# Stick-breaking attention of four heads: values projected together, the next head's queries and keys between the items, diagonal items on fewer columns

## The reference, cut to what matters

```python
q, k, v = [t.reshape(bsz, s, SB_HEADS, SB_HEAD_DIM) for t in jnp.split(qkv, 3, axis=-1)]   # qkv = h @ w_in
q, k = rms_norm_2(q, q_norm_g), rms_norm_2(k, k_norm_g)
# for blocks of 128 queries and 128 keys, from the diagonal outwards (o = 0, 1, ...):
z = jnp.einsum("bhnqd,bhnkd->bhnqk", qb[:, :, o:], kb[:, :, :n])     # qb is scaled by d ** -0.5
log_beta = jax.nn.log_sigmoid(z)
log_keep = log_beta - z
if o == 0: log_keep = jnp.where(diag_mask, log_keep, 0.0)
after = jnp.einsum("bhnqj,js->bhnqs", log_keep, suffix) + acc[:, :, o:, :, None]
att = jnp.exp(log_beta + after)
if o == 0: att = jnp.where(diag_mask, att, 0.0)
out = out.at[:, :, o:].add(jnp.einsum("bhnqk,bhnkd->bhnqd", att, vb[:, :, :n]))
acc = acc.at[:, :, o:].add(jnp.sum(log_keep, axis=-1))
```

## Time and profile before

| | us |
|---|---|
| median of 3 runs | 5148.59 (5147.55 to 5153.25) |
| profiled execution, its time | 5148.16 |
| profiled execution, its span | 5146.3 |
| the stage of the change, from its first load to the next stage's | 2812.3 to 3272.3 |

### The profile page before, as it was taken

The page is one execution under the profiler, slowest core; times in us unless marked ns, Lnnn a source line. Parts: engine busy times, 40 slices in busy tenths (PEclk is TensorE's granted clock), DMA queues, the critical chain, the costliest instruction groups (busy, mean ns, idle before and its releaser), DMA issues. The chain is left out here.

```text
span 5146.3 us, 45404 instructions
## 1 busy us (share of the span) xinstructions
PE 4150.6 (81%) x17034; PEld 2982.0 (58%) x17034; DVE 2160.6 (42%) x2568; ACT 1483.9 (29%) x2331; POOL 890.4 (17%) x386
## 2 busy tenths in 40 slices
PE   6698699978696899777667888874699875799996
PEld 6576455557574455555446555553477764566663
DVE  0293366632463676322374111315212202566665
ACT  1211245531112445210313333312210101455551
POOL 0142300002343000023110111120234322100001
PEclk6799799989898899888888998986799985899997
DMA  4111112222111021123221101220233230799995
GB/s 147 57 37 31 31 65 83 74 84 96 33 43 39 25 68 55 62 78 37 38 49 45 13 12 12 23 26 0 25 43 49 31 131 35 280 379 380 379 346 217
DMA packets 351721, 470.70 MB, mean 91 GB/s; under 512 B 46301, under 2 KB 217282, under 8 KB 351042
## 3 DMA queue, kind: packets, MB, share of 16 engines
q1 hardware_dynamic: 338770, 423.88, 28.4%
q0 software_dynamic: 7888, 26.78, 1.4%
q10 hardware_dynamic: 4896, 17.83, 0.9%
HBM read 396.59 MB, written 71.86 MB: 91 GB/s over the span
## 5 line engine op out<-in xcount | busy, mean ns | idle before, releaser
L1089 PE MATMUL values<-probs,vp 128*128 128x512 f32 x672 | 348.9, 601 | 12.0 <-issue 6.4
L1178 ACT ACTIVATE probs<-scores 128x512 f32<-128x512 f32 (+1 forms) x336 | 196.1, 584 | 309.2 <-PE scores L211 307.5
L1387 POOL TENSOR_TENSOR out_hi<-out_w,ones 128x1024 fp32r<-128x1024 f32 x24 | 57.3, 2388 | 1197.6 <-DMA out_w<-in_w_out 1197.6
L209 PE MATMUL scores<-q_hi,k_rest 97*128 97x512 f32 (+1 forms) x336 | 262.4, 781 | 0.0
L676 DVE SCALAR_TENSOR_TENSOR conv_out<-conv_in,vectors,conv_out 128x1295 f32<-128x1295 f32 (+1 forms) x120 | 254.3, 2119 | 4.3
L2927 PE MATMUL dp<-h_t,abt 128*128 128x512 f32 x544 | 241.9, 597 | 1.9 <-ACT abt L2975 1.9
L209 PE MATMUL gates_ps<-x_t_r,gates_w_r 128*128 128x512 f32 (+1 forms) x560 | 210.3, 376 | 22.0 <-POOL gates_w_r L257 22.0
L209 PE MATMUL out_ps<-h_t_r,out_w_r 128*128 128x512 f32 (+1 forms) x448 | 172.2, 384 | 67.8 <-POOL out_w_r L1389 67.8
L2957 ACT ACTIVATE expert_hi<-wu 128x1024 fp32r<-128x1024 f32 x136 | 144.9, 1065 | 253.2 <-PE gp L211 253.2
L1260 DVE TENSOR_REDUCE mx<-made 128x1 f32<-128x640 f32 (+1 forms) x272 | 203.6, 793 | 27.1 <-PE made L1030 26.5
L210 PE MATMUL gates_ps<-h_t_r,gates_hi 128*128 128x512 f32 (+1 forms) x560 | 209.9, 375 | 0.0
(11 more groups left out here) (517 smaller groups left out, 10247.6 us busy)
## 6 DMA issues: line engine op xcount, KB each, us to landing
wg<-in_w_gate SPq DMA_DIRECT2D x34, 2048.0 KB, 10.1
wu<-in_w_up SPq DMA_DIRECT2D x34, 2048.0 KB, 11.7
h_t<-in_w_down SPq DMA_DIRECT2D x34, 2048.0 KB, 10.1
slot_rows<-zero_rows SPq DMA_DIRECT2D x16, 1536.0 KB, 9.7
ahead_w<-in_w_ada SPq DMA_DIRECT2D x48, 512.0 KB, 3.8
slot_rows<-yb ACTq DMA_DIRECT2D x34, 512.0 KB, 8.1
gates_w<-in_w_in SPq DMA_DIRECT2D x28, 512.0 KB, 3.9
mod_w<-in_w_mod SPq DMA_DIRECT2D x12, 1024.0 KB, 5.1
```

The lines of the kernel that those rows point to most:

```text
L209: nc.tensor.matmul(out, lhs[1], rhs[0], start=start, stop=False, **kw)
L1089: nc.tensor.matmul(O[b % 2][:, 0:w], vp[g // 2 % 2][:, kb, g % 2 * VD:g % 2 * VD + P], pr[m % 3][:, 0:w], start=kb == 0, stop=kb == nk - 1 ...
L1178: nc.scalar.activation(pr[m % 3][:, 0:w], S[m % 2][:, 0:w], ACT.Exp, scale=scale).then_inc(s.exped, 1)
```

## The change

One stage takes the place of the mask stage and the loop. All instructions are written out; there is no hardware loop and no barrier between heads.

1. **Values.** `v` of all four heads is projected first, from chunks of 128 input rows by 512 columns of weights (256 KB): ACT rounds a chunk, DVE makes the rest, and TensorE does 24 matmuls on 512 columns for it (8 token blocks in 8 PSUM banks, 8 chunks one after the other). Chunks 4 to 7 are loaded into the places of chunks 0 to 3 when TensorE has used those. ACT copies each bank to `sb_v`.
2. **Next head's queries and keys.** The 12 items of each head are numbered on through all heads (48). At items 0, 3, 6 and 9 of heads 0 to 2, TensorE projects one piece of the next head between the product of item n+2 and the sums of item n; its square, norm sum, root and norm are at later places of ACT, PE and DVE (`piece_at`). Weights of the next head are loaded into columns of `k.x` that hold context tokens, when the third and fourth piece of the head before have been projected; GpSimd splits them as before, now beside the items.
3. **Columns.** For a diagonal item, product, softplus, sums, exp and weighing start at column `col0(n)`, so they cover 128, 256, 384 and 512 columns for the four items of a half. The mask is applied to 128 columns only. The accumulator matmul covers 128 columns fewer than the item, and the last item of a half updates no accumulator.
4. The mask is loaded beside the values, 2 x 128 columns of it in place of 2 x 896.

```diff
-        with nc.Fori(0, SB_HEADS) as h, stage(nc, names) as s, nc.Block() as block, ExitStack() as es:
+    items = [(h, qb, kb) for h in range(H) for qb in range(2) for kb in range(4 * qb + 3, -1, -1)]
+    PIECES = [(0, 0), (1, 0), (0, 1), (1, 1)]
+    def col0(n):
+        return P * max(items[n][2] - 4 * items[n][1], 0)
+    def piece_at(n):
+        if n < 0 or n >= NI - per_head or n % 3:
+            return None
+        return 4 + 4 * (n // per_head) + n % per_head // 3
...
+            for j in range(4):                                    # SP
+                sp.dma_start(v_raw(j), w3[:, j, 2, :]).then_inc(v_in[j], 16)
+            for x in range(2):
+                sp.dma_start(w_raw(x), w3[:, :, x, 0:P]).then_inc(w_in_sem[x], 16)
+            for j in range(4, DK):
+                sp.wait_ge(s.v_used, j - 3)
+                sp.dma_start(v_raw(j), w3[:, j, 2, :]).then_inc(v_in[j % 4], 16)
...
+            for h in range(1, H):
+                for x in range(2):
+                    sp.wait_ge(s.projected, 4 * (h - 1) + 3 + x)
+                    sp.dma_start(w_raw(x), w3[:, :, x, h * P:(h + 1) * P]).then_inc(w_in_sem[x], 16)
...
+            for j in range(DK):                                   # TensorE
+                pe.wait_ge(s.v_rest, j + 1)
                 for t in range(NT2):
-                    for j in range(DK):
-                        m = split_matmul(nc, bank[4 + t // 4][:, (t % 4) * P:(t % 4 + 1) * P],
-                                         split_h(k, j, CTX + t * P, P), part(j, 2), start=j == 0, stop=j == DK - 1)
+                    m = split_matmul(nc, bank[t][:, :], split_h(k, j, CTX + t * P, P), (v_hi(j), v_rest(j)),
+                                     start=j == 0, stop=j == DK - 1)
+            def project(p):
+                h, i = divmod(p, 4)
+                x, b = PIECES[i]
+                pe.wait_ge(s.split, 4 * h + 2 * x + 2)
+                if p < 4:
+                    pe.wait_ge(s.v_kept, p + 1)
+                else:
+                    pe.wait_ge(s.normed, p)
+                for j in range(DK):
+                    m = split_matmul(nc, piece_out(p)[:, :], (w_hi(x)[:, j, :], w_rest(x)[:, j, :]),
+                                     split_h(k, j, X_BLOCKS[b][0], 512), start=j == 0, stop=j == DK - 1)
...
+            for n in range(NI):
+                if n + 2 < NI:
+                    product(n + 2)
+                if piece_at(n) is not None:
+                    project(piece_at(n))
+                sums(n)
+                if piece_at(n - 1) is not None:
+                    norm_sum(piece_at(n - 1))
+                if n:
+                    weigh(n - 1)
...
+            for n in range(NI):                                   # ScalarE
+                if n + 1 < NI:
+                    soft(n + 1)
+                act.wait_ge(s.summed_up, n + 1)
+                if n >= 2:
+                    act.wait_ge(s.weighed, n - 1)
+                c = col0(n)
+                nc.scalar.activation(att[n % 2][:, c:512], bank[n % 4][:, c:512], ACT.Exp).then_inc(s.exped, 1)
+                if piece_at(n) is not None:
+                    square(piece_at(n))
+                if piece_at(n - 1) is not None:
+                    root(piece_at(n - 1))
+                if n >= 2 and last(n - 2):
+                    keep(n - 2)
...
+                if piece_at(n - 2) is not None:                   # VectorE, at the end of item n
+                    norm(piece_at(n - 2))
```

More of the change, by code:

```diff
@@ new lines, in acc_ops @@
+    def acc_ops(n):
+        return 0 if last(n) else int(diag(n)) + int(not first(n))
+    diags = [sum(diag(i) for i in range(n + 1)) for n in range(NI)]
+    accs = [sum(acc_ops(i) for i in range(n + 1)) for n in range(NI)]
+    def piece_at(n):
+        if n < 0 or n >= NI - per_head or n % 3:
+            return None
+        return 4 + 4 * (n // per_head) + n % per_head // 3
+    names = ("v_in0 v_in1 v_in2 v_in3 q_in k_in mask_in rounded scaled v_rounded v_rest v_used v_made v_kept split projected squared "
+             "summed logged rooted normed z_made absed expneg logp softplus masked summed_up exped weighed acc_step o_kept")
@@ new lines, in sums @@
+            def sums(n):
+                o, c = bank[n % 4], col0(n)
+                if diag(n):
+                    if n == 0:
+                        pe.wait_ge(s.rounded, 2)
+                    pe.wait_ge(s.masked, diags[n])
+                    nc.tensor.matmul(o[:, c:c + P], ident_r[:, :], mask_r[:, :], start=False, stop=False, skip_group_check=True)
+                else:
+                    pe.wait_ge(s.softplus, n + 1)
+                if not first(n):
+                    pe.wait_ge(s.acc_step, accs[n - 1])
+                    ca = c + P if diag(n) else 0
+                    nc.tensor.matmul(o[:, ca:512], k.mats[:, NEG_ONES, :], acc[(n - 1) % 2][:, ca:512], start=False, stop=False,
+                                     skip_group_check=True)
+                nc.tensor.matmul(o[:, c:512], k.mats[:, NEG_FROM, :], sp_[n % 2][:, c:512], start=False, stop=True,
+                                 skip_group_check=True).then_inc(s.summed_up, 1)
@@ new lines, in weigh @@
+            def weigh(n):
+                h, qb, kb = items[n]
+                o, c, v = out_bank[qb], col0(n), vt[:, kb, h * P:(h + 1) * P]
+                pe.wait_ge(s.exped, n + 1)
+                if first(n):
+                    if h:
+                        pe.wait_ge(s.o_kept, 2 * (h - 1) + qb + 1)
+                    else:
+                        pe.wait_ge(s.v_kept, NT2)
+                m = nc.tensor.matmul(o[:, c:512], v, att[n % 2][:, c:512], start=first(n), stop=last(n), skip_group_check=True)
+                m.then_inc(s.weighed, 1)
@@ new lines, in _ @@
+            project(0)
+            project(1)
+            norm_sum(0)
+            project(2)
+            norm_sum(1)
+            project(3)
+            norm_sum(2)
+            product(0)
+            product(1)
+            norm_sum(3)
+            for n in range(NI):
[8 more added lines that the diff above has]
+                    weigh(n - 1)
```

337 lines of the change are left out of this document (163 added, 174 removed).

## The result

| | before | after |
|---|---|---|
| median, us | 5149.0 (4 runs, 5147.55 to 5153.25) | 4935.74 (4 runs, 4933.43 to 4938.53) |
| ratio | | 0.9583, 95% interval 0.9569 to 0.9597 |
| profiled span, us | 5146.3 | 4931.6 |
| the attention stage, first load to the next stage's | 460.0 | 282.4 |

The stage itself came out near the forecast (282.4 for about 286). The surplus came from stages that the change doesn't touch.

What follows compares the result with a forecast made beforehand. TensorE was taken to bound each head wherever it has work, waiting between for weights and normalization. Work of 268.3 us plus waits made 283.3 for 457.6 us, a gain of 174.3: 4974 us, range 4960 to 5008.

Steps and rivals of the forecast that it cites:

- The stage lies alone between barriers, so what it saves the program saves.: Attention stage, 460.0 us of the 5146.3 us span: its whole saving, 174.3 us, was taken as the program's.
- Start and values: Stage's opening: 4.3 us to the first matmul, then 192 value matmuls of 0.233 us, 44.7 us.
- slow clock: TensorE's slow matmuls after idling: paid in each head before, now only once; 1.5 us taken.
- gap at chunk 4: Value matmuls: chunks 4 to 7 load under three chunks, 16.8 us, so no wait; at most 48 us if uncovered.
- Weights of head 1: Ahead of the fifth piece: TensorE waits for head 1's weights and head 0's last norm; 3 us taken.
- Items and pieces: Heads 1 and 2 with their pieces about 57 us each; a head's items 30.1 us, item 0 waits 0.7.
- Splits beside VectorE: 12 GpSimd splits beside items delay VectorE: 2 us in sum taken, bounded by 0 and 28 us.
- A gap where GpSimd splits: Sign of being wrong: TensorE shows gaps where GpSimd splits the next heads' weights beside items.
- The first: Rival, 10%: ACT and DVE set the narrow items, so fewer columns bring nothing; 45 us dearer, 5019 us.
- the second: Rival, 12%: GpSimd's splits stop VectorE and with it TensorE; 28 us less the 2 taken, 5000 us.
- The third: Rival, 3%: TensorE is granted the lower clock through the stage, all 268 us double; 5242 us.
- The sum to TensorE's end: Attention stage, start to TensorE's end: 268.3 us of TensorE work plus uncovered waits, 283.3 us; 457.6 before.

Runs made afterwards that it cites:

- pad8_after: An unused 8.5 MB input allocated ahead of all others, against the kernel after with a count clamped to at least 1; 4974.1 us.
- c_before: The kernel before with only the count of expert turns clamped to at least 1, as a control; 5147.6 us, ratio 0.9995.
- pitch_wide: The kernel after, with w_in_2 first copied in 16 parts to rows 43520 bytes apart, which the second block reads; 4922.1 us.
- no_narrow: The kernel after with every item on all 512 columns, diagonal ones too; 4970.6 us, attention stage 321.4 us.
- values_128: The kernel after with values made by 768 matmuls on 128 columns in place of 192 on 512; 5090.8 us, attention stage 399.0.
- pitch_late: pitch_wide with its 16 copies issued by ScalarE inside the first block's attention, behind each head's fifth exponential; 4880.7 us.
- code_before: The kernel before with 459 idle one-column matmuls added in the program's first stage; 5313.6 us, ratio 1.0328.

## Why the prediction was right and wrong

**What failed** is the step "The stage lies alone between barriers, so what it saves the program saves." It took the stages outside as unchanged. They gave 37 us, because the loads of `w_in_2` are cheaper in the changed program. With equally dear or equally cheap loads on both sides the gain is 173.5 or 170.7 us, where the sum had 174.3. That pad8_after took 4974.1, the forecast to the digit, is in part luck: against c_before its stage saved 182.3 us where 174.3 were summed, and its gdn began 7 us later. With cheap loads on both sides the stage saved 169.3. The step also took the stage's own saving as fixed, and it depends on the loads as well, since the kernel before waits for `sb_w` in each head.

**Start and values.** 4.3 + 44.7 + 1.5 us of slow clock, 50.5; measured 50.4 to the first piece (4.5 and 45.9). No gap at chunk 4.

**Weights of head 1.** 3 us taken; 2.06 + 0.71 idle, both until a norm was done. The last norm ended at 2885.71 and the second split of the queries at 2884.89, about as late as each other, as the prediction had it. Missed: TensorE came back at the slow clock, and the fifth piece's first matmuls are some 0.43 us apart until 2888.95. That is 1.6 us, more than the 1.1 by which this head (56.7) is longer than the next (55.6); the prediction had the slow clock paid once.

**Items and pieces.** 22.4 + 3.4 + 30.1 + 0.7 = 56.6 a head; measured 55.6, without the 0.7 of waiting at item 0. In head 3 the waits are 1.2 + 0.3 us, 1.2 were taken.

**Splits beside VectorE.** 2 us taken, 28 as the bound. No wait of TensorE is put down to GpSimd in the kernel after, but six of the twelve splits beside items met a VectorE instruction. In one GpSimd was the slower, 2.92 us for 2.36:

```profile
2926.66 2.92 POOL L2212 TENSOR_TENSOR x_t_r<-x_t,h_t_r 128x1024 fp32r<-128x1024 f32 x1
```

In five it was VectorE: mask multiplies of 1.80, 2.30 and 1.33 us where the others take 0.29, an accumulator add of 2.72 for 0.69 and an accumulator copy of 2.30 for 0.22, 8.7 us more in sum. Each ended 0.1 to 0.5 us behind the split it met. The first, ahead of the last norm of head 0:

```profile
2882.54 2.35 POOL L2212 TENSOR_TENSOR x_t_r<-x_t,h_t_r 128x1024 fp32r<-128x1024 f32 x1
2883.24 1.80 DVE L2408 TENSOR_TENSOR sb_sp<-sb_sp,sb_mask 128x128 f32<-128x128 f32 x1
2884.97 0.74 DVE L2388 SCALAR_TENSOR_TENSOR sb_qk<-sbb,vectors,sb_rt 128x512 f32<-128x512 f32 x1
```

It is the one that TensorE felt: the 2.06 us ahead of the fifth piece lie here. In pitch_wide, where the weights land sooner and this multiply takes 0.29 us, the same wait is 1.26, so the collision cost some 0.8 us. The other four fell where TensorE had work. A gap where GpSimd splits was one of the prediction's signs of being wrong; it came, and was small.

**Rivals.** The first is out by no_narrow. Of the second the first half is true, the splits do stop VectorE; that they stop TensorE for their whole length is out, at 0.8 us for 28. The third, the lower clock through the stage, did not come; but values_128 shows that it can, on the values alone.

The sum to TensorE's end was 283.3 us. Measured is 280.3 (2805.68 to 3086.0, with the same 0.2 us taken off the last record). The 3 us between them are the net of these small terms, some above and some below; no run parts them.

## What to carry to other kernels

Before a surplus or a loss is put down to an edit, compare the stages that it doesn't touch; if they moved, shift the data (an unused input), by more than one size, and time both kernels again: here 1 MB moved little and 8.5 MB much. Compare the landing of equal loads from different tensors in one trace: 8 us beside 3.9 for the same packets was to be seen before any change, and another row spacing took 55 us more off the time. A background copy was free where no load behind it was waited for (pitch_late); ahead of 16 stages it cost 41 us more, and in two bursts ahead of urgent loads 69. Where two engines share work beside each other, look for instructions that take several times their usual length, even if no wait names the other engine.

## What the runs showed of the hardware

- Loads of 512 KB in packets of 512 bytes (median of `gates_w`, `gdn_w`, `ssm_w` or `merge_w`) landed in 3.8 to 4.0 us from rows 43520 or 10880 bytes apart, and in 6.0 to 9.0 us from rows 32832 bytes apart, there differing between programs whose code for them is the same. No run tries a fourth spacing.
- Six of twelve GpSimd splits of 2.4 us overlapped a VectorE instruction that reads SBUF, and one of the two lasted longer than usual. Five times it was VectorE's: instructions of 0.22 to 0.69 us took 1.33 to 2.72 us and ended just behind the split. Four of the five read two SBUF operands, the copy of 2.30 us one.
- TensorE ran dense matmuls on 128 columns at 1.2 GHz for the whole of 120 us (values_128, granted clock 0.50), with the clock down when they began; in the kernel after the same values on 512 columns got 2.4 GHz after 4 us. In the kernel before 192 matmuls on 128 columns stood 0.112 us apart for 21.5 us, with the clock up when they began.
- A plain f32 matmul on one column took 0.43 us (196 us for 459), twice the 0.22 of one on 128 columns, at a granted clock of 1.00. The trace of the kernel before had this too: 192 such matmuls on two columns, at its start, took 82 us (59.9 to 141.6), also 0.43 each, at a granted clock of 0.50. A window over the idle matmuls of code_before, PE and PEld alone (two records a matmul, 140 us for 643):

```profile
60.00:200.00 140.00, 137.04 (x643) 136.95 (x642) 1.00 0.01 3
```

- What decides whether a program gets the dear or the cheap loads stays open: unused inputs and idle matmuls in the first stage both move it, and no run shows an address.
